# Expert stage of a two-layer diffusion trunk: gathers of U one head ahead of V, loops unrolled

## The reference, cut to what matters

```python
def block(xb):
    qry = (xb @ wq).reshape(n, 8, 2, 64)                      # 8 heads
    s1 = einsum('nhd,hkd->nhk', qry[:, :, 0], sub_keys[:, 0])  # 128 scores
    s2 = einsum('nhd,hkd->nhk', qry[:, :, 1], sub_keys[:, 1])  # 128 scores
    v1, i1 = top_k(s1, 16);  v2, i2 = top_k(s2, 16)
    cand = v1[..., :, None] + v2[..., None, :]                 # 256 pair sums
    sc, pos = top_k(cand, 16)
    idx = (i1[..., :, None] * 128 + i2[..., None, :]) taken at pos
    g = softmax(sc)
    act = gelu(einsum('nd,nhkd->nhk', xb, peer_u[idx]))
    return einsum('nhk,nhkd->nd', (g * act), peer_v[idx])
```

## Time and profile before

| | |
|---|---|
| median of the runs | 5119.65 us |
| span of the profiled execution | 5121.3 us |
| PE busy in the span | 3764.5 us (74%) |
| DVE | 2862.3 us (56%) |
| POOL | 2687.4 us (52%) |
| ACT | 1063.2 us (21%) |
| software DMA queue | 1342.34 MB, 69.8% of 16 engines |

### The profile page before, as it was taken

How to read it: one execution, slowest core, us unless ns; L and a number is a source line. 1 busy time by engine, 2 the same in 40 slices (tenths; PEclk the granted TensorE clock), 3 DMA queues, 4 the chain that set the end, 5 groups by cost and what they waited for, 6 DMA issues and landing times.

```text
span 5121.3 us, 48248 instructions
## 1 busy us (share of the span) xinstructions
PE 3764.5 (74%) x12022; PEld 1932.4 (38%) x12034; DVE 2862.3 (56%) x6385; ACT 1063.2 (21%) x2469; POOL 2687.4 (52%) x2761
## 2 busy tenths in 40 slices
PE   7897867676767767676668978666766676677666
PEld 3465533333333333333324555333333333333332
DVE  2524455656565565656645363566666656666664
ACT  1123111221121121122121241112212221222221
POOL 2700045565566565666656300566666666666665
PEclk8998688888888888888889977888888888888888
DMA  5122269999999999999981102799999999999998
GB/s 172 31 76 83 75 238 339 358 343 352 344 356 356 344 361 335 358 348 358 364 334 39 47 2 75 269 366 362 349 358 366 363 355 361 366 356 359 355 367 312
DMA packets 512066, 1453.42 MB, mean 284 GB/s; under 512 B 52896, under 2 KB 171108, under 8 KB 511844
## 3 DMA queue, kind: packets, MB, share of 16 engines
q0 software_dynamic: 368640, 1342.34, 69.8%
q1 hardware_dynamic: 143336, 109.91, 6.8%
HBM read 1448.83 MB, written 3.24 MB: 284 GB/s over the span
## 4 chain that ended last, share of the span: by engine, by line
PE 41%; DMA 21%; issue 20%; POOL 9%; DVE 6%; ACT 2%; POOLq 1%; SPq 0%; DVEq 0%; ACTq 0%
PE ps L536 39%; DMA arena<-in_peer_u,rows_for_u 21%; POOL arena L519 6%; POOL arena L527 3%; DVE arena L1362 1%; PE ps L640 1%; DVE arena L1283 1%; ACT arena L1072 1%; POOLq L517 0%; DVE expert_weight L1369 0%; ACT expert_gelu L1058 0%; DVE arena L1266 0%; DVE arena L1296 0%; DVE gate_rec L1367 0%; DVE arena L1171 0%
## 5 line engine op out<-in xcount | busy, mean ns | idle before, releaser
L536 PE MATMUL ps<-arena 128*128 128x512 f32 (+7 forms) x9648 | 3407.6, 518 | 1189.5 <-ACT arena L1072 1140.9
L536 PEld LDWEIGHTS ps<-arena 128*128 128x128 f32 (+3 forms) x9648 | 1701.3, 206 | 2825.9 <-issue 1553.0
L1362 DVE CUSTOM_DVE_ANT_0 arena<-arena,ps 128x1024 f32<-128x1024 f32 x1280 | 1562.9, 1221 | 1321.4 <-DMA arena<-in_peer_u,rows_for_u 1272.4
L527 POOL DMA_INDIRECT arena<-in_peer_v,rows_for_v x1280 | 1214.1, 948 | 1028.1 <-PE ps L536 806.5
L519 POOL DMA_INDIRECT arena<-in_peer_u,rows_for_u x1280 | 1200.1, 938 | 583.1 <-issue 429.6
L1072 ACT ACTIVATE arena<-constants,expert_weight 128x128 f32<-128x128 f32 x1280 | 475.5, 396 | 953.0 <-PE ps L536 892.8
L1058 ACT ACTIVATE expert_gelu<-expert_act 128x16 f32<-128x16 f32 x80 | 17.3, 216 | 1264.7 <-DVE expert_act L1362 1264.7
L1211 DVE TENSOR_REDUCE score_max<-ps 128x1 f32<-128x640 f32 (+1 forms) x80 | 57.4, 718 | 302.9 <-PE ps L536 302.9
L504 POOL MEMSET arena<- 128x5632 f32 x2 | 9.6, 4792 | 405.7 <-ACTq L258 405.7
L536 PE MATMUL ps<-arena,cond_silu 128*2 128x128 f32 (+1 forms) x1344 | 186.7, 294 | 19.2 <-DMA arena<-in_ada_w 11.9
L497 POOL TENSOR_SCALAR arena<-arena,vec_columns 128x512 f32<-128x512 f32 x120 | 153.0, 1286 | 10.5 <-issue 10.5
(11 more groups left out here) (163 smaller groups left out, 1894.5 us busy)
## 6 DMA issues: line engine op xcount, KB each, us to landing
arena<-in_ada_w SPq DMA_DIRECT2D x80, 512.0 KB
arena<-in_peer_u,rows_for_u POOLq DMA_INDIRECT x1280, 6.5
arena<-in_peer_v,rows_for_v POOLq DMA_INDIRECT x1280, 6.1
arena<-in_w_in SPq DMA_DIRECT2D x32, 512.0 KB, 4.0
arena<-in_ada_w SPq DMA_DIRECT2D x4, 2048.0 KB, 17.1
arena<-in_w_out SPq DMA_DIRECT2D x4, 2048.0 KB, 7.7
arena<-in_peer_wq SPq DMA_DIRECT2D x2, 4096.0 KB, 18.1
peer_modulation<-modulation_rows SPq DMA_DIRECT2D x4, 1536.0 KB, 11.2
```

What stands on the lines that cost most here:

```text
L527: pool.indirect_dma_start(VR[:, k % RING, :], None, v_rows, bass.IndirectOffsetOnAxis(ap=idx_v[:, k:k + 1], axis=0))\
L536: return pe.matmul(out, lhsT, rhs, start=start, stop=stop)
L1362: dve.tensor_tensor_reduce(out=UR[:, k % RING, :], in0=UR[:, k % RING, :], in1=pair(1), scale=1.0, scalar=0.0, op0=ALU.mult, op1=ALU.add, ...
```

## The change

The expert stage is rewritten for all engines, still with the same rings of 8, 8 and 4 buffers. POOL gathers U of head 0, then in turn the 16 rows of U of head g+1 and the 16 rows of V of head g. The indices, the gate exponentials and their sums of 4 heads are kept (`LIVE = 4`), so the copy of the indices for V is gone. PE computes the query already transposed (operands swapped), so the transpose and its copy are gone; query and scores are now made three heads ahead, before rows 0 and 5 of the V loop. The first and last real matmul of a tile open and close the PSUM sum, so the zero matmuls are gone. DVE routes head g+2 between dots 7 and 8 of head g. ACT does the gelu of head g+1 after the last diagonal of head g, and the exponential of head g+3 before diagonal 13 of head g. All loops over heads and tiles are written out. The work between tiles moves behind the dots of heads 1 and 2.

```diff
 POOL
-                with pool.Fori(0, NT * HEADS) as i:
-                    ... (16 U gathers of head i, then 16 V gathers of head i)
+                for k in range(TOPK):
+                    gather_u(0, k)
+                for g in range(T):
+                    if g + 1 < T:
+                        for k in range(TOPK):
+                            gather_u(g + 1, k)
+                    for k in range(TOPK):
+                        gather_v(g, k)
```

```diff
 PE
+            def query(l, g):
+                h = g % HEADS
+                if T * l + g:
+                    pe.wait_ge(S["q_ready"], T * l + g)
+                for k in range(KT):
+                    m = mm(PS[:, 6, 0:P], WQ[:, k, P * h:P * h + P], H2T[:, k, :], k == 0, k == KT - 1)
+                m.then_inc(S["q_ps"], 1)
+            def key_scores(l, g):
+                pe.wait_ge(S["q_ready"], T * l + g + 1)
+                if T * l + g:
+                    pe.wait_ge(S["sc_now"], T * l + g)
+                mm(PS[:, 4, 0:256], QT, KEYS[:, g % HEADS, :]).then_inc(S["sc_ps"], 1)
+            def peer(l):
+                pe.wait_ge(S["res_read"], NT * (l + 1))
+                query(l, 2)
+                key_scores(l, 2)
+                for g in range(T):
+                    t, h, n = g // HEADS, g % HEADS, T * l + g
+                    if h == 0 and NT * l + t:
+                        pe.wait_ge(S["acc_out"], NT * l + t)
+                    if h == HEADS - 3 and t + 1 < NT:
+                        tile_transposes(l, t + 1)
+                    for k in range(TOPK):
+                        if l == 0 and t < 4 and h < 6 and k in (4, 14):
+                            ... (mod_block)
+                        if g + 3 < T:
+                            if k == 0:
+                                query(l, g + 3)
+                            if k == 5:
+                                key_scores(l, g + 3)
+                        pe.wait_ge(v_in[k % RING], n * 32 + 16 * (k // RING + 1))
+                        pe.wait_ge(S["diag_ready"], n * TOPK + k + 1)
+                        ... (two matmuls)
+                        m.then_inc(S["v_free"], 1)
```

```diff
 ACT
+                for g in range(T):
+                    t, h, n = g // HEADS, g % HEADS, T * l + g
+                    if h == HEADS - 3 and t + 1 < NT:
+                        tile_out(l, t + 1)
+                    act.wait_ge(S["w_ready"], n + 1)
+                    for k in range(TOPK):
+                        if g + 3 < T:
+                            if k == 2:
+                                query_out(l, g + 3)
+                            if k == 7:
+                                scores_out(l, g + 3)
+                            if k == 13:
+                                gate_exp(l, g + 3)
+                        ... (mod_rows at k 6 and 15)
+                        if n * TOPK + k >= DIAGS:
+                            act.wait_ge(S["v_free"], n * TOPK + k + 1 - DIAGS)
+                        ... (diagonal k)
+                    if g + 1 < T:
+                        expert_gelu(l, g + 1)
+                    ... (after head 7: copy of the tile)
```

```diff
 DVE
+            def head_dots(l, g):
+                n = T * l + g
                 for k in range(TOPK):
-                    if k == 9:
-                        dve.wait_ge(S["v_free"], head * TOPK + RING)
-                        dve.tensor_copy(idx_v[:, :], idx_u[:, :]).then_inc(S["idxv_ready"], 1)
+                    if k == 8 and g + 2 < T:
+                        route(l, g + 2)
                     ... (dot k)
+                dve.wait_ge(S["exp_done"], n + 1)
+                dve.reciprocal(grec[:, :], gsum[:, g % LIVE:g % LIVE + 1])
+                dve.wait_ge(S["gelu_done"], n + 1)
+                ... (weights, w_ready)
             def peer(l):
+                route(l, 1)
+                for g in range(T):
+                    t, h = g // HEADS, g % HEADS
+                    if h == 0:
+                        ... (copy of the token tile to PSUM)
+                    head_dots(l, g)
+                    if h == 1 and t + 1 < NT:
+                        normed(l, t + 1)
+                    if h == 2 and t:
+                        residual(l, t - 1)
+                residual(l, NT - 1)
```

More of the change, by code:

```diff
@@ new lines, in gather_u @@
+                def gather_u(g, k):
+                    n = T * l + g
+                    if k == 0:
+                        pool.wait_ge(S["idx_ready"], n + 1)
+                    if n * TOPK + k >= RING:
+                        pool.wait_ge(S["u_free"], n * TOPK + k + 1 - RING)
+                    pool.indirect_dma_start(UR[:, k % RING, :], None, u_rows,
+                                            bass.IndirectOffsetOnAxis(ap=rows[:, g % LIVE, k:k + 1], axis=0))\
+                        .then_inc(u_in[k % RING], 16)
@@ new lines, in gather_v @@
+                def gather_v(g, k):
+                    n = T * l + g
+                    if n * TOPK + k >= RING:
+                        pool.wait_ge(S["v_free"], n * TOPK + k + 1 - RING)
+                    pool.indirect_dma_start(VR[:, k % RING, :], None, v_rows,
+                                            bass.IndirectOffsetOnAxis(ap=rows[:, g % LIVE, k:k + 1], axis=0))\
+                        .then_inc(v_in[k % RING], 16)
+                for k in range(TOPK):
+                    gather_u(0, k)
@@ L830, in out_project @@
-                key_scores(g + 1, 1)
+                key_scores(l, 1)
                 mix(4, 1)
[L833 to L852, removed]
@@ L854, in peer @@
             def peer(l):
                 pe.wait_ge(S["res_read"], NT * (l + 1))
[L856 to L867, removed]
-                        tile_transposes(l, t + 1)
[L869 to L876, removed]
+                query(l, 2)
@@ L1036, in gla, with query_out @@
                         .then_inc(S["og_sd"], 1)
[L1038 to L1049, removed]
+            def query_out(l, g):
+                n = T * l + g
+                act.wait_ge(S["q_ps"], n + 1)
+                if n:
+                    act.wait_ge(S["sc_ps"], n)
+                act.activation(QT, PS[:, 6, 0:P], ACT.Copy).then_inc(S["q_ready"], 1)
@@ L1050, in scores_out @@
+            def scores_out(l, g):
+                n = T * l + g
+                act.wait_ge(S["sc_ps"], n + 1)
+                if n:
+                    act.wait_ge(S["sc_taken"], n)
                 act.activation(SCC[:, :, :].rearrange("p a b -> p (a b)"), PS[:, 4, 0:256], ACT.Copy)\
                     .then_inc(S["sc_now"], 1)
[L1053 to L1057, removed]
-                act.activation(gelu_h[:, :], act_h[:, :], ACT.Gelu).then_inc(S["gelu_done"], 1)
[L1059 to L1069, removed]
-                    act.wait_ge(S["v_free"], head * TOPK + k + 1 + RING - DIAGS)
-                    act.activation(DG[:, k % DIAGS, :], ident, ACT.Copy, scale=w_h[:, k:k + 1])\
-                        .then_inc(S["diag_ready"], 1)
@@ new lines, in gate_exp, with expert_gelu @@
+            def gate_exp(l, g):
+                n = T * l + g
+                act.wait_ge(S["idx_ready"], n + 1)
+                if n >= LIVE:
+                    act.wait_ge(S["w_ready"], n - LIVE + 1)
+                act.activation(gexp[:, g % LIVE, :], centred[:, :], ACT.Exp,
+                               accum_out=gsum[:, g % LIVE:g % LIVE + 1]).then_inc(S["exp_done"], 1)
+            def expert_gelu(l, g):
+                act.wait_ge(S["u_free"], (T * l + g + 1) * TOPK)
+                act.activation(gelu_h[:, :], act_h[:, :], ACT.Gelu).then_inc(S["gelu_done"], 1)
@@ L1113, in peer @@
             def peer(l):
-                for t in range(NT):
-                    n = NT * l + t
-                    with act.Fori(0, HEADS - 2) as i:
-                        head_weights(HEADS * n + i, True, 12 * t + i * 2 if l == 0 and t < 4 else None)
-                    if t + 1 < NT:
-                        tile_out(l, t + 1)
-                    with act.Fori(0, 2) as i:
-                        head_weights(HEADS * n + HEADS - 2 + i, t + 1 < NT)
-                    act.wait_ge(S["acc_done"], n + 1)
-                    if n:
-                        act.wait_ge(S["y_ready"], n)
-                    act.activation(TMP, pair(0), ACT.Copy).then_inc(S["acc_out"], 1)
+                query_out(l, 2)
+                scores_out(l, 2)
+                gate_exp(l, 1)
+                gate_exp(l, 2)
+                expert_gelu(l, 0)
+                for g in range(T):
+                    t, h, n = g // HEADS, g % HEADS, T * l + g
+                    if h == HEADS - 3 and t + 1 < NT:
+                        tile_out(l, t + 1)
+                    act.wait_ge(S["w_ready"], n + 1)
[7 more added lines that the diff above has]
+                                gate_exp(l, g + 3)
+                        if l == 0 and t < 4 and h < 6 and k in (6, 15):
+                            block = 12 * t + 2 * h + k // 10
```

(31 more changed lines are left out.)

113 lines of the change are left out of this document (35 added, 78 removed).

## The result

The kernel after takes 5460.9 us (median of 4 runs, 5452.7 to 5479.1) against 5118.9 us on the same chip: a ratio of 1.067, 95% interval 1.065 to 1.070. It is slower by 342 us where 399 were forecast, and the time lies in the forecast range.

The account below looks back on a forecast made before the run. No engine was taken as the limit; a head is a sequence of waits. The new loop's terms make 51.7 us a turn against 46.8, 54.7 in modulation heads; layers +217 and +182 give 5518 us, range 5,400 to 5,650.

Parts of the forecast that it names:

- w to the issue of U gather 15: Loop from a head's weights ready: dots 0 to 7 of the next head 10.3 us, then 0.5 to POOL's issue.
- V gather 0 to PE's start: Loop: one more POOL issue, 1.2 us, then landing and PE start, 6.1 us, the median of all V gathers.
- PE's start to ACT's copy of the scores: Loop: PE's V rows up to the scores product before row 5, half-clock start included, 11.6 us.
- copy, wake and route: Loop: ACT copies the scores and DVE wakes, 0.5 us; DVE's route, formerly beside PE's work, 10.2 us.
- dots 8 to 15 and the way to the weights: Loop on DVE behind the route: eight dots 10.3 us, then last dot to weights ready 0.9 us.
- Work between tiles: Copy, `normed` and `residual`, five DVE operations now between weights and next dots: 26 us a layer, all on the path.
- Modulation heads: Layer one's heads with modulation blocks: first block adds 3.0 us before row 5, 54.7 us a turn; second block stays covered.
- ACT's branch: Last diagonal, table load, gelu, weights after PE's start: 25.8 us against 33.5 on DVE's way, so not binding.
- A: Rival: scores are there when DVE asks, POOL's turn of 45.3 us binds; 5,125 us, no change; 3%.
- B: Rival: both gather streams overlap and transfers bind at 409 GB/s, 41 us a head; about 4,650 us; 2%.
- C: Rival: same loop, but landing near 9 us or the exponential's cover gone; 54.7 us a turn, 5,750 us; 10%.
- The costs put at nothing: Removed zero matmuls, transpose and copies lie in idle time; unrolled loops priced at nothing, bounds 24 us gained or lost.

Follow-up runs that it names:

- the first experiment: The changed kernel with PE's scores of head g+3 moved from before row 5 to before row 0 of V, ACT's copies with them: 5078.4 us, ratio 0.992.

## Why the prediction was right, by its steps

The mechanism was the one forecast, and three runs bear it out from different sides: take PE's product ahead of the wait and the loss goes; take the dots from behind the wait and it goes; put the product three rows later and it grows by three rows a turn. The other candidates are out as causes of the loss: the mean clock hardly differs between a version at 5,461 and one at 5,078, and a change of order alone brought all the time back. The slow start of PE's block is inside the 11.6 us below, but it was in the 11.2 us before as well; no run takes it away while the loop stands. What no run takes apart is how much of the landing of V gather 0 is its own time and how much the gathers ahead of it.

The terms, as medians over 35 turns of layer two in the trace of after:

- w to the issue of U gather 15: 10.84, forecast 10.8. The size is right by luck. Dots 0 to 7 take 1.14 us each, not 1.28, and dot 7 ends after 9.1; but U gathers 8 to 15 follow dot 0 at POOL's own 1.24 us apart (4222.66 to 4231.35 in the chain), so POOL is late where I had DVE, by about as much.
- V gather 0 to PE's start: 1.24 + 6.73, forecast 1.2 + 6.1. The landing was 0.6 too low. For all V gathers issue to landing is 6.3 us (median) after, 6.1 before.
- PE's start to ACT's copy of the scores: 11.63, forecast 11.6.
- copy, wake and route: 0.41 + 10.2, forecast 0.5 + 10.2. The first MAX8 is preceded by some 22 us of idle time, 20 forecast; that is 1,660 us in total. This is the step on which the sign hung.
- dots 8 to 15 and the way to the weights: 9.8, forecast 10.3 + 0.9. This term was mis-sized by 1.4 us, 1.2 of them in the dots. Rows 8 to 15 landed while DVE waited and routed, so the dots go 1.14 apart, while the earlier trace rows held the landing's pace of 1.28. I read a pace as a duration.

A turn without tile work is 51.16 us (mean of 24), where 51.7 were carried: the dots gave back 1.4 us and the landing, 6.9 in these turns, took 0.8 of them. Over 37 turns the 0.5 us left are about 20 us of layer two.

**Work between tiles** was the other mis-sized term: 26 us a layer forecast, about 9 measured (37 intervals sum to 1902 us; 37 x 51.16 taken off). The turn that holds the copy is as long as the others, those with `normed` and `residual` are 0.7 and 1.5 us longer. U gather 15 is issued only 0.8 us later behind the copy and 1.7 later behind the two pairs, though dot 0 starts 1.5 and 2.5 us later: POOL's pace covers the rest, and the landings behind the copy and behind `normed` are shorter (6.1 and 6.4 us). I had put them wholly on the path.

These two make 37 of the 38 us by which layer two was forecast too high. Its start (60.6 us to PE's first V row, 61.3 forecast) and its end hold. In layer one +166.6 stands against +182. Modulation heads took 55.0, 54.7 forecast, and that is in part luck. PE's start to ACT's copy of the scores was 13.7 there (mean of 24), 2.1 above the 11.6 of ordinary heads, where 3.0 were forecast for the first block. V gather 0 took 8.2 us to land, not 6.1, which made up for the dots. The forecast had put the loads of the slabs outside the path; they are the likely reason for the longer landing, as the rows of V took 6.7 in layer two, but no run takes them away. The weights never waited for the second block, which stayed covered.

One printed sum is short of a term: 23.6 - 0.4 + 1.3 + 0.9 for ACT's branch make 25.4; the 25.8 take in the last diagonal's own 0.40.

**The rivals.** A (scores in time, POOL binds at 45.3, 5,125 us) was untrue of this kernel, but it is what the first experiment makes: 45.0 us and 5,078. ACT's branch, 25.8 + 18.1 = 43.9 by the forecast's terms, ends last there in 29 heads of 38, and POOL's turn in the other 9. B (transfers bind, 4,650 us) was right in its mechanism and wrong only in its condition: interleaved gathers meet it, at 4,717. Its windows of 400 us stand at 398 and 407 GB/s; the 358 GB/s of the Trainium skill ("DMA: Bandwidth & Descriptors", section "Bandwidth"), which the page also gives as the share of a core while both cores of a pair stream, did not bind with one core at work. C (landings near 9 us) did not come: they were 6.7 in layer two and 8.2 in modulation heads. The 3.2 us that the Trainium skill's fit for one DMA comes to for 512 KB, an estimate (the same page, section "Anatomy of one DMA — SWDGE (gpsimd) path"), were met by no V gather of either kernel; the shortest took 3.9 and 4.1 us.

**The costs put at nothing.** Branch or no branch made 12 us of loss when taken alone, inside the bounds given (24 gained to 24 lost). Zero matmuls, transpose and index copy weren't tried alone; the experiments that keep them away and change only the order go from 4,717 to 5,847, so they don't decide here.

## What to carry to other kernels

When a pipeline is set up over an in-order engine, follow every wait back to its own releaser through all the queues; if the way round comes back to the same engine one head earlier, add up its terms, because that sum is the turn, whatever the engines' busy shares say. Place work for a later stage ahead of a wait, not behind it, and put what other engines wait for ahead of an instruction that waits: either edit alone took back over 350 us here (382 and 355), and issuing two streams by turns instead of in blocks of 16 took 744. And read an even spacing as a pace before taking it for a cost: compare it with the bytes and the rate.

## What the runs showed of the hardware

- The 128x1024 product with its sum on DVE lasts 1.22 us and starts again 1.14 us later when its rows are there; 1.28 between starts is the landing of 0.524 MB at 409 GB/s. The waits of 0.14 us between them don't show in the timeline as idle time.
- One core's 16 DMA engines kept up 398 to 407 GB/s over windows of 400 us of indirect gathers, with a busy share of 1.02 to 1.03, and 412 in the best window of 8 us.
- The granted clock was 0.50 in the window in which PE idled for 8 us, 0.81 in the next one, and 1.00 over the 400 us from 3200 of the interleaved kernel, in which PE had no long gap. These are the levels 1.2 and 2.4 GHz and a mean of the two.
- Writing out the loops over heads cost 0.3% (5130.9 against 5118.5 us), with the bytes of the page's two instruction queues going from 0.87 to 1.64 MB and from 0.30 to 1.11 MB.
